# A two-block transformer on one Trainium2 core: VectorE takes six taps of GpSimd's last convolution tile, and the opening is cut into pieces with identity transposes on TensorE

## The reference, cut to what matters

```python
h = _rmsnorm(x, norm_mix_g)                  # the opening: norm, then the first projection
proj = h @ w_in
p_a, p_b, q, p_g = jnp.split(proj, IN_SPLITS, axis=-1)
u, ug = jnp.split(p_b, 2, axis=-1)
u = u * jax.nn.sigmoid(ug)
u = _causal_dwconv(u, conv_b_w) + conv_b_bias    # depthwise, 31 taps, 1024 channels
u = jax.nn.silu(_layernorm(u, ln_b_g, ln_b_b))
y_b = u @ w_b_out
# beside it: memory attention, 4 heads, whose queries, keys and values are split into parts
s = jnp.einsum("bshd,bmhd->bhsm", qh, kh)
```

## Time and profile before

| | |
|---|---|
| median of three runs | 1187.89 us |
| profiled execution, whole / span of its instructions | 1190.51 / 1188.4 us |
| TensorE matmul busy | 1150.7 us, 97% of the span |
| VectorE / ScalarE / GpSimd busy | 842.3 / 613.6 / 482.8 us |
| mean granted TensorE clock | 0.988 |

### The profile page before, as it was taken

One profiled execution on the slowest core, in us unless ns is written; L12 is line 12 of the kernel. 1 busy time (PEld: TensorE's weight loads), 2 busy tenths in 40 slices (PEclk: granted clock), 3 DMA queues, 4 the chain that ended last, 5 costly groups with the idle time before them and its releaser, 6 DMA issues.

```text
span 1188.4 us, 19024 instructions
## 1 busy us (share of the span) xinstructions
PE 1150.7 (97%) x7297; PEld 1038.7 (87%) x7297; DVE 842.3 (71%) x1066; ACT 613.6 (52%) x829; POOL 482.8 (41%) x411
## 2 busy tenths in 40 slices
PE   6999999997999999999998999999999999999997
PEld 6999999886999999999897888888888788888885
DVE  5688988983676688888788775665666576655655
ACT  6544434564554554455567764444454577434443
POOL 1699997997200222331323628880010355000000
PEclk9999999998999999999999999999999999999999
DMA  8555555552266465555343277555555403655550
GB/s 292 177 180 181 194 170 196 178 195 88 72 198 204 158 199 189 178 175 204 119 163 109 72 198 249 196 180 198 190 165 189 171 25 127 210 178 187 200 177 36
DMA packets 142616, 201.06 MB, mean 169 GB/s; under 512 B 3236, under 2 KB 123044, under 8 KB 142556
## 3 DMA queue, kind: packets, MB, share of 16 engines
q1 hardware_dynamic: 141312, 195.83, 49.7%
q0 software_dynamic: 912, 3.17, 1.2%
q10 hardware_dynamic: 332, 1.25, 0.3%
HBM read 199.20 MB, written 1.05 MB: 169 GB/s over the span
## 4 chain that ended last, share of the span: by engine, by line
PE 81%; POOL 7%; DVE 6%; ACT 3%; issue 2%; DMA 1%; ACTq 0%; SPq 0%; POOLq 0%; DVEq 0%
PE ps L1827 55%; PE ps L1867 13%; PE ps L1870 6%; POOL work L542 3%; PE ps L1945 3%; POOL misc L546 3%; DVE wlo L1131 1%; PE ps L2007 1%; ACT whi L637 1%; DVE work L1391 1%; PE ps L1866 1%; DMA raw<-in_w_in 1%; PE ps L1995 1%; DVE ps L1339 1%; ACT ps L724 0%
## 5 line engine op out<-in xcount | busy, mean ns | idle before, releaser
L1131 DVE TENSOR_TENSOR wlo<-raw,whi 128x2048 fp32r<-128x2048 f32 (+2 forms) x165 | 380.1, 2304 | 151.4 <-ACT whi L637 151.4
L637 ACT ACTIVATE whi<-raw 128x2048 fp32r<-128x2048 f32 (+2 forms) x180 | 341.3, 1898 | 198.4 <-PE ps L1827 188.4
L1827 PE MATMUL ps<-p_parts,whi 128*128 128x256 f32 x1616 | 293.5, 284 | 2.1 <-DVE p_parts L1157 2.1
L1867 PE MATMUL ps<-p_parts,whi 128*128 128x512 f32 x832 | 291.0, 398 | 1.7 <-DVE p_parts L1157 1.7
L1827 PEld LDWEIGHTS ps<-p_parts,whi 128*128 128x128 f32 x1616 | 254.0, 193 | 3.3 <-issue 1.9
L1827 PE MATMUL ps<-p_parts,wlo 128*128 128x256 f32 x808 | 229.5, 284 | 0.0
L1870 PE MATMUL ps<-p_parts,wlo 128*128 128x256 f32 x728 | 204.3, 281 | 0.0
L1867 PEld LDWEIGHTS ps<-p_parts,whi 128*128 128x128 f32 x832 | 151.6, 188 | 31.6 <-issue 1.6
L469 POOL TENSOR_TENSOR wlo<-raw,whi 128x2048 fp32r<-128x2048 f32 x14 | 65.1, 4647 | 229.1 <-ACT whi L637 229.1
L1827 PEld LDWEIGHTS ps<-p_parts,wlo 128*128 128x128 f32 x808 | 155.8, 193 | 0.0
L1827 PE MATMUL ps<-whi,q_hi 128*128 128x512 f32 x380 | 148.6, 391 | 1.4 <-DVE q_lo L1544 1.4
(11 more groups left out here) (302 smaller groups left out, 1828.3 us busy)
## 6 DMA issues: line engine op xcount, KB each, us to landing
raw<-in_w_in SPq DMA_DIRECT2D x36, 1024.0 KB, 4.9
raw<-in_w_up SPq DMA_DIRECT2D x22, 1024.0 KB, 5.0
raw<-in_up_a SPq DMA_DIRECT2D x16, 1024.0 KB, 5.5
raw<-in_down_a SPq DMA_DIRECT2D x16, 1024.0 KB, 5.0
raw<-in_up_b SPq DMA_DIRECT2D x16, 1024.0 KB, 5.4
raw<-in_down_b SPq DMA_DIRECT2D x16, 1024.0 KB, 4.9
raw<-in_od_w_qkv SPq DMA_DIRECT2D x12, 1024.0 KB, 5.2
raw<-in_w_down SPq DMA_DIRECT2D x11, 1024.0 KB, 4.7
```

Of the source, the lines that this page charges most:

```text
L637: nc.scalar.activation(whi[:, g % R, 0:n], raw[:, g % R, 0:n], ACT.Copy).then_inc(hi_ready, 1)
L1131: nc.vector.tensor_tensor(wlo[:, g % R, 0:n], raw[:, g % R, 0:n], whi[:, g % R, 0:n].bitcast(F32), ALU.subtract).then_inc(lo_ready[g % R], 1)
L1827: ins = nc.tensor.matmul(dst, lhs, rhs, start=first and n == 0, stop=last and n == 2)
L1867: ins = nc.tensor.matmul(dst, whi[:, r, at], p_parts[:, :, S * k:S * k + S], start=k == 0, stop=k == KD - 1)
```

## The change

Two independent edits.

The tail. GpSimd stops tile 4 after 25 of its 31 taps (`POOL_TAPS` is now 87 in place of 93). VectorE computes the last six into the two halves of bank 7 (`conv_tail`, six instructions, between the last but one and the last weight group of the gate stage), and adds the two partial sums to GpSimd's (`conv_joined`, two adds, between the row maxima of head 0 and its division). TensorE's wait for the taps counts these.

The opening. Weight group 0 is loaded in four pieces (256 KB each) and split piece by piece: all four upper pieces by ScalarE, the first lower piece by VectorE, the other three by GpSimd; the first product waits piece by piece. The first half of `xn` is now made by ScalarE as soon as its root is there, the second by VectorE. `mem` is loaded by SP behind the third weight group. VectorE's lower part of group 0 is gone from before `norm_lower`, but for one quarter. TensorE turns the identity against itself (9 transposes before `vecs`, 9 after, 1 after `cwf`), and transposes `cwf` before `x` in place of after it.

```diff
+TAIL = 6
+POOL_TAPS = K_B * len(CONV_POOL) - TAIL
 # SP
-            for j, c0 in enumerate((3 * D, 4 * D, 5 * D)):
+            for n in range(4):
+                first = raw[:, 0, BW * n:BW * n + BW].rearrange("p (k n) -> p k n", k=2)
+                sp.dma_start(first, cols("w_in", 3 * D)[:, 2 * n:2 * n + 2, :]).then_inc(raw_in[0] if n == 3 else first_in[n], 16)
+            for j, c0 in ((1, 4 * D), (2, 5 * D)):
                 load(G_UGQ + j, cols("w_in", c0), KD)
+            sp.dma_start(mem_rows, d["mem"].rearrange("(t p) n -> p t n", p=P)).then_inc(mem_in, 16)
 # GpSimd
             inverse_root("n_mix")
+            for n in range(1, 4):
+                if n < 3:
+                    pool.wait_ge(first_hi, n + 1)
+                else:
+                    pool.wait_ge(hi_ready, 1)
+                    pool.wait_ge(first_lo, 1)
+                part = slice(BW * n, BW * n + BW)
+                nc.gpsimd.tensor_tensor(out=wlo[:, 0, part], in0=raw[:, 0, part], in1=whi[:, 0, part].bitcast(F32),
+                                        op=ALU.subtract).then_inc(lo_ready[0] if n == 3 else first_lo_pool, 1)
...
-                for k in range(K_B):
+                for k in range(K_B - TAIL if c == CONV_POOL[-1] else K_B):
 # ScalarE
-            act.wait_ge(x_in[1], 16)
-            act.dma_start(mem_rows, d["mem"].rearrange("(t p) n -> p t n", p=P)).then_inc(mem_in, 16)
-
             act.wait_ge(vec_tr, 1)
             nc.scalar.activation(vec[:, :], bank(0, 0, KD * NV), ACT.Copy).then_inc(bank_read[0], 1)
+            act.wait_ge(norm_r, 1)
+            nc.scalar.activation(xn[:, 0, :], x[:, 0, :], ACT.Copy, scale=rr[:, 0:1]).then_inc(first_rows, 1)
             act.wait_ge(bank_read[0], 1)
-            hi(0)
+            for n in range(4):
+                act.wait_ge(raw_in[0] if n == 3 else first_in[n], 16)
+                part = slice(BW * n, BW * n + BW)
+                nc.scalar.activation(whi[:, 0, part], raw[:, 0, part], ACT.Copy).then_inc(hi_ready if n == 3 else first_hi, 1)
 # VectorE
-            normalise("n_mix", x, False)
-            lo(0)
+            first_mean_square(1)
+            dve.wait_ge(norm_r, 2)
+            nc.vector.tensor_scalar(xn[:, 1, :], x[:, 1, :], rr[:, 1:2], None, ALU.mult).then_inc(norm_xn, 2)
+            dve.wait_ge(first_hi, 1)
+            nc.vector.tensor_tensor(wlo[:, 0, 0:BW], raw[:, 0, 0:BW], whi[:, 0, 0:BW].bitcast(F32), ALU.subtract).then_inc(first_lo, 1)
...
+            def conv_tail():
+
+                c, base = CONV_POOL[-1], TAPS * len(CONV_DVE)
+                dve.wait_ge(conv_tap, base)
+                for n in range(TAIL):
+                    k = K_B - TAIL + n
+                    src, w = misc[:, c * UP + k:c * UP + k + S], gain(V_CONVB + k, c)
+                    if n < 2:
+                        nc.vector.tensor_scalar(acc[n], src, w, None, ALU.mult).then_inc(conv_tap, 1)
+                    else:
+                        dve.wait_ge(conv_tap, base + n - 1)
+                        nc.vector.scalar_tensor_tensor(out=acc[n % 2], in0=src, scalar=w, in1=acc[n % 2],
+                                                       op0=ALU.mult, op1=ALU.add).then_inc(conv_tap, 1)
+
+            def conv_joined():
+
+                c, base = CONV_POOL[-1], TAPS * len(CONV_DVE) + TAIL
+                dst = conv[:, c * S:(c + 1) * S]
+                dve.wait_ge(pool_tap, POOL_TAPS)
+                for n in range(2):
+                    dve.wait_ge(conv_tap, base + n)
+                    nc.vector.tensor_tensor(dst, acc[n], dst, ALU.add).then_inc(conv_tap, 1)
...
+                    if 3 * i + j == 10:
+                        conv_tail()
...
             maxima("att1", 0)
+            conv_joined()
             divided("att1", 0)
 # TensorE, the first product
-                pe.wait_ge(lo_ready[g % R], g // R + 1 + i)
+                if g or after != "n_mix":
+                    pe.wait_ge(lo_ready[g % R], g // R + 1 + i)
...
+                        if after == "n_mix" and h == 0 and k % 2 == 0:
+                            done, n = ((first_lo, 1), (first_lo_pool, 1), (first_lo_pool, 2), (lo_ready[0], 1))[k // 2]
+                            pe.wait_ge(done, n)
...
+            def turn_identity(count):
+
+                for n in range(count):
+                    nc.tensor.transpose(bank(6, P * (n % 4), P * (n % 4) + P), ident[:, :], ident[:, :])
+
+            turn_identity(9)
             pe.wait_ge(vec_in, 16)
...
             last.then_inc(vec_tr, 1)
+            turn_identity(9)
+            pe.wait_ge(cwf_in, 16)
+            for k in range(K_F):
+                last = nc.tensor.transpose(bank(5, FT * k, FT * (k + 1)), cwf_rows[:, P * k:P * k + P], ident[0:FT, 0:FT])
+            last.then_inc(vec_tr, 1)
+            turn_identity(1)
             transpose_norm("n_mix")
...
-            pe.wait_ge(conv_tap, (K_B + 1) * len(CONV_DVE))
-            pe.wait_ge(pool_tap, K_B * len(CONV_POOL))
+            pe.wait_ge(conv_tap, (K_B + 1) * len(CONV_DVE) + TAIL + 2)
+            pe.wait_ge(pool_tap, POOL_TAPS)
```

More of the change, by code:

```diff
@@ L224, in two_blocks @@
         vec_tr = sem("vec_tr")
+        first_in, first_hi = [sem(f"first_in{n}") for n in range(3)], sem("first_hi")
+        first_lo, first_lo_pool, first_rows = sem("first_lo"), sem("first_lo_pool"), sem("first_rows")
         norm_sq, norm_ms, norm_r = sem("norm_sq"), sem("norm_ms"), sem("norm_r")
@@ L1302, in woven_heads, with first_mean_square @@
                     lo_half(G_F2A, 1)
-            dve.wait_ge(norm_sq, 1)
+            def first_mean_square(t):
+                dve.wait_ge(norm_sq, t + 1)
+                nc.vector.tensor_scalar(ms[:, t:t + 1], sm[:, t:t + 1], 1.0 / D, EPS, ALU.mult, ALU.add).then_inc(norm_ms, 1)
+            first_mean_square(0)
             dve.wait_ge(x_in[1], 16)
@@ L1311, in _ @@
                                     ALU.mult).then_inc(vec_fin, 1)
-            for t in range(T):
-                dve.wait_ge(norm_sq, t + 1)
-                nc.vector.tensor_scalar(ms[:, t:t + 1], sm[:, t:t + 1], 1.0 / D, EPS, ALU.mult, ALU.add).then_inc(norm_ms, 1)
-            normalise("n_mix", x, False)
-            lo(0)
+            first_mean_square(1)
[3 more added lines that the diff above has]
+            nc.vector.tensor_tensor(wlo[:, 0, 0:BW], raw[:, 0, 0:BW], whi[:, 0, 0:BW].bitcast(F32), ALU.subtract).then_inc(first_lo, 1)
             norm_lower("n_mix", p_hi, p_lo)
@@ L1911, in transpose_norm @@
                 for t in range(T):
-                    pe.wait_ge(norm_xn, T * m + t + 1)
+                    if name == "n_mix" and t == 0:
+                        pe.wait_ge(first_rows, 1)
+                    else:
+                        pe.wait_ge(norm_xn, T * m + t + 1)
                     for c in range(KD):
@@ L2106, in memory @@
                     to_rows(G_KV + 4 + i, 2, q_pair, 2 * i, 3, 2, BW, i == 0, i == 3)
-            pe.wait_ge(cwf_in, 16)
-            for k in range(K_F):
-                last = nc.tensor.transpose(bank(5, FT * k, FT * (k + 1)), cwf_rows[:, P * k:P * k + P], ident[0:FT, 0:FT])
-            last.then_inc(vec_tr, 1)
             for j in range(3):
```

## The result

The changed kernel takes 1176.24 us (median of four runs, 1175.76 to 1176.85) against 1188.61 of the kernel before beside it (1187.63 to 1189.92). Between the two medians that is 12.4 us. By the ratio, 0.9892 with a 95% interval of 0.9880 to 0.9904, it is 12.8 us or 1.1% less, 11.4 to 14.3 by the interval. The profiled execution took 1176.07 us, with a span of 1174.1 us against 1188.4.

The account below looks back on a forecast made before the run. TensorE, busy nearly throughout, bounds the kernel through waits and slow clock. Gains of 3.0 + 1.6 + 8.1 + 2.5 = 15.2 us from 1187.89, with half the 1.6 taken, gave 1173.5 us; range 1170.5 to 1177.0.

Parts of the forecast that it names:

- The stall: Before head 1's scores: TensorE's 8.1 us wait on GpSimd goes, plus 2.5 us of slow clock behind it.
- The spare time: Before head 1's scores: GpSimd's lower parts end at 278.3, TensorE needs them at 280.1, 1.8 us to spare.
- The cover of the tail: VectorE's gap before 270.77: six taps cost 2.4 us, move a gate half by 1.0, free within 0.2.
- The start of the first product: In the opening: first product at about 12.9 in place of 15.94, 3.0 us earlier.
- the first pair is there by 10.8: In the opening: TensorE's transposes of `x`, 0.11 to 0.22 us each, give the first pair by 10.8, before 11.2.
- GpSimd's three quarters: Group 0's lower part in the opening: three pieces on GpSimd, 1.23 us each, from 10.2 to 13.9, free.
- `mem` and group 1: Opening loads: `mem` lands near 19.5 without harm; group 1 lands at 13.3, its lower part made by 18.4.
- The tight place: Group 1's lower part ready at 18.4, TensorE needs it at 18.7: 0.3 us to spare.
- The clock of the opening: Turned identity raises the clock before `x` is transposed, no fall behind: 1.6 us gained; rival of a fall, chance 0.17.
- Half of the 1.6: Opening's clock gain: only half taken for the median, since the fall need not occur in every execution before.
- The rule I had set against the change: In the opening: transposes don't count as busy for the clock, so the first product would begin at 1.2 GHz.
- The sum: Whole kernel: 3.0 + 1.6 + 8.1 + 2.5 = 15.2 us; 1173.5 forecast for the median.

Follow-up runs that it names:

- the tail alone: The kernel before with only six taps and two adds moved from GpSimd to VectorE: 1178.28 us, ratio 0.9902.
- the variance split: The changed kernel with the variance's 32 one-column matmuls cut into two 16s, transposes and scores between: 1173.17 us, ratio 0.9870.
- the opening alone: The changed kernel with all 31 taps of the last tile back on GpSimd: 1186.35 us, ratio 0.9977 against the kernel before.
- the two traces with the late rise: The changed kernel with group 0's four lower pieces all on VectorE (1176.33 us), and with `mem` loaded by ScalarE's queue as before (1176.60 us).
- full products from 3.1 on: The changed kernel with the 19 identity transposes replaced by 19 products of `mean_w` with itself: 1176.88 us, ratio 0.9881.
- the second group of runs: The changed kernel unaltered, measured again on the same chip as other variants: 1175.19 us, ratio 0.9879 against the kernel before (1189.30).
- `mem` early: The changed kernel with `mem` loaded by ScalarE's queue behind the second half of `x`, as before: 1176.60 us, ratio 0.9887.

## Why the prediction was right, and where it was not

**The stall.** Predicted 8.1 of waiting and 2.5 of clock, 10.6; measured 10.9 between the two traces, 10.7 between those of the tail alone and before, 11.0 in medians and 11.7 by the ratio. The terms are right in kind and size. The spare time was not 1.8 us but 0.9: GpSimd's lower parts were done at 275.47 (274.16 + 1.31) and TensorE came at 276.37. Its last tap ended at 272.97, where the earlier trace rows less the shift of 3.6 would have been 271.8. As many steps were stretched beside VectorE's splits as before (five in the last part of tile 4), but they took 2.85 to 2.96 each, where three of the five took 2.20 to 2.80 before. Three taps left on GpSimd brought 3.0 us of waiting back.

**The cover of the tail.** Six taps were to take 2.4 in VectorE's gap; they took 2.4 (265.77 to 268.19). The gate half behind them began at 268.11, 0.9 later than the earlier trace rows less 3.6, as counted (1.0), and the split behind that at 268.77, no later than 272.57 less 3.6. The join took 0.87 and had 2.8 us to spare before the mean at 277.80. No wait of TensorE came in its place.

**The start of the first product.** Predicted 3.0 earlier, measured 2.3. The failed step is "the first pair is there by 10.8": it gives the transposes 0.11 to 0.22 us each, and for the first eight to be done when the second half of `xn` comes (10.4) they must take less than the 0.22 that the earlier trace rows has for them in this place. Eight of them plus two of the second half took 2.23 from 9.52 on, the pair was there at 11.75, and ScalarE waited 0.43 us for it. ScalarE's upper parts ended at 11.35 and not 11.2, and its two gain copies and VectorE's pair took 0.1 each more than counted: 0.7 in all. The load in pieces carried its share, without it the start was 0.7 to 1.0 later, and `mem`'s new queue another 0.6. One reading was wrong without bearing on the sum: 8.84 in the earlier trace rows is when the two power steps began, not when the roots were there.

**GpSimd's three quarters.** "1.23 each, from 10.2 to 13.9": they took 4.34, to 14.7, and VectorE's quarter 1.76 and not 0.6, because the two engines collided. It cost nothing in this trace, since TensorE came to the last one at about 15.8. It can cost something: in the trace with the variance split the clock rose at 10.5, the transposes of `x` were done sooner, and the chain to the first product (13.30) passes VectorE's quarter instead:

```profile
10.73 1.68 DVE wlo L1339
```

What GpSimd's help bought is about half a microsecond, by the estimate above.

**`mem` and group 1.** Predicted to land at 19.5 and to be ready at 18.4 for a need at 18.7; `mem` was issued at 7.52 and landed at 7.52 + 11.7 = 19.2, group 1's lower part was ready at 18.9, and TensorE wanted it at 19.4. The tight place held with 0.5 us.

**The clock of the opening.** This step was wrong in its reason. I had the rise "before `x` is transposed" and the level held by the turned identity. The identity transposes all ran at the lower level, the rise came at 11.6, and without any turning it came at 12.5 with no fall behind it either. In two traces with the turning in place the level was still down at 18. The size had a wrong reading in it too: 16.91 to 20.32 is not the time of the first 48 matmuls, of which the earlier trace rows counts 18 there. The first weight group took from 15.94 to 23.24, 7.3 us against 5.8 without the fall (13.62 to 19.44), so the fall cost 1.5. That the changed kernel's trace shows no slow stretch there is a matter of the execution, and so was the fall in the trace of before. Half of the 1.6 was taken for the median; the opening alone gave 2.7 by its ratio, and with 2.3 of it from the start 0.4 is left for the clock, half of what was taken and with an interval (1.4 to 3.9 for the 2.7) that can't tell the two apart.

The rule I had set against the change (the Trainium skill, TensorE: Matmul & The Clock Gate, Part 4, PE-mode transpose: transposes don't count as busy for the clock) would have given the first product at the lower level. The traces are divided on it. Without the turning there is nothing but transposes of `x` between 9.0 and the rise at 12.5, which speaks against the rule. But in the two traces with the late rise the same sixteen transposes ran from 9.7 to 13.3 and from 10.0 to 13.7, all at the lower level, and the rise came only 4 to 5 us behind the start of the first product (18.4 and 18.9), which is what the rule would give. For the identity the traces agree with its result, but full products from 3.1 on did no better, so the rule isn't shown as the cause. What raises the clock in the opening stays open.

**The sum.** 14.4 us were forecast for the median, 12.8 measured by the ratio (11.4 to 14.3). For the same kernel in the second group of runs it was 14.4 by the ratio (12.2 to 16.4) and 14.1 between the medians. Of the shortfall of 1.6, 0.7 is the start; the rest is within what the slow stretches of single executions move. The forecast of 1173.5 was taken from a median of before of 1187.89, which was 0.7 to 2 us below the later ones.

## What to carry to other kernels

When an engine with slow steps is late at one rendezvous, count its last steps back from the waiting engine's own time, give exactly those to an engine with a gap, and look at what the wait did to the clock behind it: 8.1 us of idle cost 10.7 in the traces. Cost an instruction by the row nearest in time and state, not by the same instruction elsewhere: a factor of two in TensorE's clock was visible in the first trace. Before claiming a few tenths of a per cent for the clock, take a second trace of the unchanged kernel.

## What the runs showed of the hardware

The granted clock. In fourteen traces TensorE's clock first rose between 10.5 and 18.9 us, never earlier, though in one of them TensorE was busy from 3.1 without a gap. Slow stretches were 3.4, 6.8 or 10.2 us long, and two executions of one kernel differed in which they had.

One-column matmuls. 32 of them in a row kept TensorE occupied for 3.5 to 4.0 us, and the clock fell during or behind them in each of twelve traces. In two groups of 16 with transposes and scores in between it did not fall there, in two traces.

VectorE and GpSimd. A subtraction of two SBUF operands of 128x512 took VectorE 0.69 us alone and 1.76 when one of GpSimd's had begun before it (10.34 and 10.54 in the changed kernel's trace). When VectorE's began first it took 0.69 (10.38, with GpSimd's from 10.65, with `mem` early). GpSimd's power step on one column took 0.56, and two took 2.04 when VectorE's square of 1.23 us ran over them. GpSimd's tap multiply took 0.92, and 2.96 beside a split of VectorE's; beside taps of VectorE that accumulate in PSUM it was not stretched. For the subtractions and the taps this agrees with the Trainium skill, SBUF — State Buffer, SBUF: two separate sides: the two engines share a port pair that one of them holds for a whole instruction while the other blocks, if VectorE reads two SBUF operands or is in a mode that takes both ports. The square reads one tensor, and no run here shows which of these cases it is.
